# Transposes between a mixer's stages: squares of 32x32 on VectorE in place of whole ones on TensorE

## The reference

```python
h = rms_norm(x, pre_g)
q_a, k_a, v_a, z_a, u_c, b_c, c_c, z_c, q_r, k_r, v_r, z_r, g_a, g_c, g_r = split(h @ w_in)
o_a = dilated_mixture_attn(q_a, k_a, v_a) * silu(z_a)          # 12 heads of 128
o_c = b_c * causal_short_conv(c_c * u_c, conv_w, conv_b) * silu(z_c)   # 1536 channels, 3 taps
o_r = retention(q_r, k_r, v_r) * silu(z_r)                     # 12 heads, q and k rotated
merged = sigmoid(g_a) * (o_a @ w_a) + sigmoid(g_c) * (o_c @ w_c) + sigmoid(g_r) * (o_r @ w_r)
x = x + rms_norm(merged @ w_out, post_g)
```

## Time and profile before

| | |
|---|---|
| median of 3 runs | 2805.48 us (2804.77 to 2805.68) |
| profiled execution | 2805.61 us, span 2803.7 us |
| mean granted clock of TensorE | 0.999 |
| matmuls on TensorE | 12744 |
| ScalarE busy | 1257.4 us, 45% |
| DMA | 189 GB/s in the mean, 56.1% of 16 engines' time; 1 MB of weights lands in 5.1 us |

### The profile page before, as it was taken

One profiled execution on the slowest core, in us unless ns is written; L12 is line 12 of the kernel. 1 busy time (PEld: TensorE's weight loads), 2 busy tenths in 40 slices (PEclk: granted clock), 3 DMA queues, 4 the chain that ended last, 5 costly groups with the idle time before them and its releaser, 6 DMA issues.

```text
span 2803.7 us, 30612 instructions
## 1 busy us (share of the span) xinstructions
PE 2785.3 (99%) x12744; PEld 2318.5 (83%) x12744; DVE 1514.7 (54%) x1663; ACT 1257.4 (45%) x1484; POOL 26.6 (1%) x35
## 2 busy tenths in 40 slices
PE   8999999999999999999999999999999999999998
PEld 7888888888888888888878888888888888888887
DVE  5554544555545666546555445445555556555465
ACT  5554544444443444444455545444444434344443
POOL 0000000000000000000000000000000000000000
PEclk9999999999999999999999999999999999999999
DMA  8555555555656555556565555555655565555563
GB/s 311 167 180 179 172 191 194 192 190 186 195 193 192 171 193 169 176 191 215 181 225 171 176 179 177 191 192 191 193 184 194 195 194 167 192 169 179 194 211 135
DMA packets 264107, 529.13 MB, mean 189 GB/s; under 512 B 8352, under 2 KB 8480, under 8 KB 263712
## 3 DMA queue, kind: packets, MB, share of 16 engines
q1 hardware_dynamic: 260208, 517.24, 56.1%
q10 hardware_dynamic: 2752, 5.05, 0.5%
q0 software_dynamic: 1008, 4.87, 0.5%
HBM read 522.94 MB, written 4.19 MB: 188 GB/s over the span
## 4 chain that ended last, share of the span: by engine, by line
PE 99%; DVE 0%; DMA 0%; ACT 0%; issue 0%; DVEq 0%; POOL 0%; ACTq 0%; POOLq 0%
PE ps L589 32%; PE ps L591 32%; PE ps L590 32%; PE ps L473 2%; PE ps L531 0%; PE ps L528 0%; PE ps L529 0%; PE ps L502 0%; PE ps L506 0%; PE ps L515 0%; DMA merged<-xT 0%; PE ps L507 0%; PE ps L501 0%; DVE gates L1068 0%; DVE hT_trail L1040 0%
## 5 line engine op out<-in xcount | busy, mean ns | idle before, releaser
L836 DVE TENSOR_TENSOR w_trail<-raw,w_lead 128x1024 fp32r<-128x1024 f32 x975 | 1192.0, 1225 | 1250.4 <-ACT w_lead L648 1248.7
L648 ACT ACTIVATE w_lead<-raw 128x1024 fp32r<-128x1024 f32 x975 | 1032.4, 1060 | 1487.2 <-PE ps L591 1479.3
L589 PE MATMUL ps<-w_lead,hT_lead 128*128 128x512 f32 x3328 | 1304.6, 392 | 10.8 <-DVE w_trail L1077 9.3
L591 PE MATMUL ps<-w_lead,hT_trail 128*128 128x512 f32 x3328 | 1296.6, 390 | 0.0
L590 PE MATMUL ps<-w_trail,hT_lead 128*128 128x512 f32 x3328 | 1296.1, 389 | 0.0
L589 PEld LDWEIGHTS ps<-w_lead,hT_lead 128*128 128x128 f32 x3328 | 625.6, 188 | 138.6 <-DVE hT_trail L1059 9.2
L591 PEld LDWEIGHTS ps<-w_lead,hT_trail 128*128 128x128 f32 x3328 | 625.3, 188 | 130.5
L590 PEld LDWEIGHTS ps<-w_trail,hT_lead 128*128 128x128 f32 x3328 | 625.8, 188 | 127.2
L589 PE MATMUL ps<-w_lead,oT_lead 128*128 128x512 f32 x576 | 224.6, 390 | 0.0
L591 PE MATMUL ps<-w_lead,oT_trail 128*128 128x512 f32 x576 | 224.1, 389 | 0.0
L590 PE MATMUL ps<-w_trail,oT_lead 128*128 128x512 f32 x576 | 224.1, 389 | 0.0
(11 more groups left out here) (96 smaller groups left out, 783.9 us busy)
## 6 DMA issues: line engine op xcount, KB each, us to landing
raw<-w_in SPq DMA_DIRECT2D x383, 1024.0 KB, 5.1
raw<-w_out SPq DMA_DIRECT2D x32, 1024.0 KB, 5.1
raw<-w_branch_a SPq DMA_DIRECT2D x24, 1024.0 KB, 5.0
raw<-w_branch_c SPq DMA_DIRECT2D x24, 1024.0 KB, 5.1
raw<-w_branch_r SPq DMA_DIRECT2D x24, 1024.0 KB, 5.0
gates<-x SPq DMA_DIRECT2D x4, 512.0 KB, 13.2
post_gain<-post_norm_g POOLq DMA_DIRECT2D x2, 1024.0 KB, 6.7
gates<-x ACTq DMA_DIRECT2D x4, 512.0 KB, 6.1
```

What stands on the lines that cost most here:

```text
L589: pe.matmul(acc, lead[:, k, tok(t)], wl, start=(k == 0), stop=False)
L591: last = pe.matmul(acc, trail[:, k, tok(t)], wl, start=False, stop=(k == BLOCKS[n][2] - 1))
L648: act.activation(w_lead[:, h % SPLIT_SLOTS, :], raw[:, i % RAW_SLOTS, part:part + HALF * COLS], ACT.Copy).then_inc(lead_ready, 1)
L836: dve.tensor_tensor(w_trail[:, s, :], raw[:, i % RAW_SLOTS, part:part + HALF * COLS], w_lead[:, s, :].bitcast(F32), ALU.subtract).then_inc ...
```

## The change

TensorE's and ScalarE's steps q, k, prod and the transposing part of out go. In their place VectorE turns the 256x512 tile (in SBUF as 128 x 2 x 512) in sixteen instructions, each of 32 partitions x 256 elements: it reads partitions 32i to 32i+31 and writes partitions 32j to 32j+31, eight squares of 32x32 each. They are dealt over six halves (`TURNS`: 3, 3, 3, 3, 2, 2), for q from 2B, for k from 3B, for prod from 2B, for z from the half behind values (attention), gate (conv and retention). The z turn writes `qT`, free by then; out reads it from there. Scores wait for the two turns. The steps behind move by one to six halves, exp from 3B+5 to 3B+7. The first piece of each turn also waits for the trails of the group before. One wait of the branch blocks is counted on `out_trail` in place of three kinds.

```diff
-STEPS = {"attention": TILES + TILES + HPB + HPB + HPB // 2 + TILES,
-         "conv": TILES + TILES,
-         "retention": TILES + TILES + HPB + HPB // 2 + TILES}
+STEPS = {"attention": HPB + HPB + HPB // 2,
+         "conv": 0,
+         "retention": HPB + HPB // 2}
...
+SQ = 32
+QUADS = P // SQ
+TURNS = ((0, 3), (3, 6), (6, 9), (9, 12), (12, 14), (14, 16))
...
+def pieces(what, at):
+    return [(what + str(i), at + i) for i in range(len(TURNS))]
...
 PE_DUE = due({
-    "attention": [("q", 2 * B + 3), ("k", 3 * B + 2), ("scores", 3 * B + 4), ("probs", 4 * B + 2),
-                  ("values", 4 * B + 4), ("out", 4 * B + 6)],
-    "conv": [("prod", 2 * B + 2), ("out", 4 * B + 2)],
-    "retention": [("q", 2 * B + 3), ("k", 3 * B + 3), ("scores", 3 * B + 5), ("values", 4 * B + 1),
-                  ("out", 4 * B + 6)]})
+    "attention": [("scores", 3 * B + 6), ("probs", 4 * B + 4), ("values", 4 * B + 6)],
+    "conv": [],
+    "retention": [("scores", 3 * B + 6), ("values", 4 * B + 2)]})
 ACT_DUE = due({
-    "attention": [("q", 2 * B + 3), ("k", 3 * B + 2), ("exp", 3 * B + 5), ("probs", 4 * B + 2),
-                  ("out", 4 * B + 6)],
-    "conv": [("prod", 2 * B + 2), ("out", 4 * B + 2)],
-    "retention": [("q", 2 * B + 3), ("k", 3 * B + 3), ("square", 4 * B + 1), ("out", 4 * B + 6)]}, AHEAD)
+    "attention": [("exp", 3 * B + 7), ("probs", 4 * B + 4), ("out", 5 * B + 4)],
+    "conv": [("out", 4 * B + 6)],
+    "retention": [("square", 4 * B + 2), ("out", 5 * B + 2)]}, AHEAD)
 DVE_DUE = due({
-    "attention": [("scores", 3 * B + 4), ("sums", 4 * B + 1), ("values", 4 * B + 4), ("out", 4 * B + 6)],
-    "conv": [("conv0", 2 * B + 3), ("conv1", 2 * B + 4), ("conv2", 2 * B + 5), ("gate", 4 * B),
-             ("out", 4 * B + 2)],
-    "retention": [("scores", 3 * B + 5), ("values", 4 * B + 1), ("norm", 4 * B + 2),
-                  ("gate", 4 * B + 3), ("out", 4 * B + 6)]}, AHEAD)
+    "attention": pieces("q", 2 * B) + pieces("k", 3 * B) + [("scores", 3 * B + 6), ("sums", 4 * B + 3),
+                 ("values", 4 * B + 6)] + pieces("z", 4 * B + 7) + [("out", 5 * B + 5)],
+    "conv": pieces("prod", 2 * B) + [("conv0", 2 * B + 6), ("conv1", 2 * B + 7), ("conv2", 3 * B),
+             ("gate", 4 * B)] + pieces("z", 4 * B + 1) + [("product", 4 * B + 6), ("out", 4 * B + 7)],
+    "retention": pieces("q", 2 * B) + pieces("k", 3 * B) + [("scores", 3 * B + 6), ("values", 4 * B + 2),
+                  ("norm", 4 * B + 3), ("gate", 4 * B + 4)] + pieces("z", 4 * B + 5) + [("out", 5 * B + 3)]}, AHEAD)
...
-                if what in ("q", "k"):
-                    i = "qk".index(what)
-                    pe.wait_ge(tables_in, 16)
-                    if mixer == "attention":
-                        pe.wait_ge(*moved_out(l, n0 + 1 + i))
-                    else:
-                        pe.wait_ge(*rotated_tiles(l, TILES * (2 * g + i + 1)))
-                    src = (q_sb, k_sb)[i]
-                    for t in range(TILES):
-                        transposes(l, m + TILES * i + t, [src[:, t, head(h)] for h in range(HPB)])
-                elif what == "prod":
-                    pe.wait_ge(*moved_out(l, n0 + 1))
-                    for t in range(TILES):
-                        transposes(l, m + t, [q_sb[:, t, head(h)] for h in range(HPB)])
-                elif what == "scores":
-                    for i in range(2 * TILES):
-                        pe.wait_ge(*step_drained(l, m + i))
+                if what == "scores":
+                    pe.wait_ge(*turned(l, "q", mixer, g))
+                    pe.wait_ge(*turned(l, "k", mixer, g))
                     for h in range(HPB):
...
+                    pe.wait_ge(tables_in, 16)
...
-                elif what == "out":
-                    s0 = m + STEPS[mixer] - TILES
-                    if mixer == "attention":
-                        for i in range(HPB // 2):
-                            pe.wait_ge(*step_drained(l, s0 - HPB // 2 + i))
-                    elif mixer == "conv":
-                        pe.wait_ge(conv_gated, l * (TILES * GROUPS) + TILES * (g + 1))
-                    else:
-                        pe.wait_ge(ret_gated, l * GROUPS + (g + 1))
-                    for t in range(TILES):
-                        transposes(l, s0 + t, [z_sb[:, t, head(h)] for h in range(HPB)])
 
...
-                    if mixer == "conv":
-                        pe.wait_ge(conv_trail, l * (TILES * GROUPS) + TILES * GROUPS)
-                    else:
-                        s = step0(mixer, GROUPS - 1) + STEPS[mixer] - TILES
-                        for t in range(TILES):
-                            pe.wait_ge(*step_drained(l, s + t))
+                    done = TILES * GROUPS * (MIXERS.index(mixer) + 1)
+                    pe.wait_ge(out_trail, l * (TILES * GROUPS * len(MIXERS)) + done)
...
-                if what in ("q", "k", "prod"):
-                    i = 1 if what == "k" else 0
-                    for t in range(TILES):
-                        s = m + TILES * i + t
-                        dst = prodT[:, :, 2 + t * P:2 + (t + 1) * P] if what == "prod" else (qT, kT)[i][:, :, tok(t)]
-                        act.wait_ge(*step_ready(l, s))
-                        act.activation(dst, heads4(side(s)[:, :]), ACT.Copy).then_inc(drained[s % SIDE_BANKS], 1)
-                elif what == "exp":
+                if what == "exp":
...
                 elif what == "out":
-                    s0 = m + STEPS[mixer] - TILES
+                    if mixer != "conv":
+                        act.wait_ge(*turned(l, "z", mixer, g))
                     for t in range(TILES):
                         dst = oT_lead[:, HPB * g:HPB * (g + 1), tok(t)]
                         if mixer == "conv":
-                            act.wait_ge(*step_drained(l, s0 + t))
-                            act.activation(dst, heads4(work2[:, t, :]), ACT.Copy).then_inc(out_lead, 1)
-                        else:
-                            lead_of_step(l, s0 + t, dst)
+                            act.wait_ge(conv_product, l * (TILES * GROUPS) + TILES * g + t + 1)
+                        act.activation(dst, out_source(mixer, t), ACT.Copy).then_inc(out_lead, 1)
...
-                if what == "scores":
+                if what[:-1] in ("q", "k", "prod", "z"):
+                    turn(l, what[:-1], mixer, g, int(what[-1]))
...
-                        for t in range(TILES):
-                            dve.wait_ge(*step_drained(l, m + t))
+                        dve.wait_ge(*turned(l, "prod", mixer, g))
...
+                elif what == "product":
+                    dve.wait_ge(*turned(l, "z", mixer, g))
+                    dve.wait_ge(conv_steps, l * (3 * HPB * GROUPS) + 3 * HPB * (g + 1))
+                    for t in range(TILES):
+                        dve.tensor_tensor(heads4(work2[:, t, :]), qT[:, :, tok(t)], kT[:, :, tok(t)],
+                                          ALU.mult).then_inc(conv_product, 1)
                 elif what == "out":
-                    s0 = m + STEPS[mixer] - TILES
-                    for t in range(TILES):
-                        s = s0 + t
-                        if mixer == "conv":
-                            dve.wait_ge(*step_ready(l, s))
-                            if t == 0:
-                                dve.wait_ge(conv_steps, l * (3 * HPB * GROUPS) + 3 * HPB * (g + 1))
-                            dve.tensor_tensor(heads4(work2[:, t, :]), heads4(side(s)[:, :]), kT[:, :, tok(t)],
-                                              ALU.mult).then_inc(drained[s % SIDE_BANKS], 1)
                     for t in range(TILES):
                         lead = oT_lead[:, HPB * g:HPB * (g + 1), tok(t)]
                         dst = oT_trail[:, HPB * g:HPB * (g + 1), tok(t)]
-                        if mixer == "conv":
-                            dve.wait_ge(*lead_steps(l, lead_no(mixer, g, t)))
-                            dve.tensor_tensor(dst, heads4(work2[:, t, :]), lead.bitcast(F32),
-                                              ALU.subtract).then_inc(conv_trail, 1)
-                        else:
-                            trail_of_step(l, s0 + t, lead_no(mixer, g, t), lead, dst)
+                        dve.wait_ge(*lead_steps(l, lead_no(mixer, g, t)))
+                        dve.tensor_tensor(dst, out_source(mixer, t), lead.bitcast(F32),
+                                          ALU.subtract).then_inc(out_trail, 1)
+
+            def turn(l, what, mixer, g, piece):
+
+                n0 = first_block(mixer, g)
+                src = {"q": q_sb, "k": k_sb, "prod": q_sb, "z": z_sb}[what]
+                if what == "prod":
+                    dst, done = prodT[:, :, 2:], prod_turned
+                else:
+                    dst, done = {"q": (qT, q_turned), "k": (kT, k_turned), "z": (qT, z_turned)}[what]
+                if piece == 0:
+                    before = l * 3 * GROUPS + group_no[mixer, g]
+                    if before > 0:
```

(52 more changed lines are left out.)

## The result

The changed kernel takes 2790.25 us in the median of 5 runs (2786.76 to 2792.14) against 2805.68 (2804.77 to 2805.90): ratio 0.9944, 95% interval 0.9932 to 0.9955, 15.4 us faster. The forecast was 2784. The runs of the kernel before that were taken beside the experiments have their medians at 2805.31 (the first four experiments) and 2805.18 (the last four); each experiment is compared with those. The profiled execution took 2791.59 us, its span is 2789.7, 14.0 under the one before.

A forecast was written before the change was run, and what follows sets the result against it. TensorE, busy 99% of the span, was taken as the bound. 42 us off for transposes, less 5 (attention's scores), 14 (retention's) and 1 (exp), gives 22 off: 2805.6 - 22 = 2784 us, range 2766 to 2818.

The forecast's parts named there:

- the gain on TensorE: 384 transposes, 48 batches of eight, leave TensorE's queue at 0.87 us each: 42 us off.
- the price of a transpose: One VectorE transpose of 32 partitions x 256 elements takes 0.44 us, between bounds of 0.36 and 0.68.
- d: Time of one VectorE transpose instruction, taken as 0.44 us without overlap, since each changes partitions.
- the filling of a square: 32 elements must be in before a square's first can leave: 0.03 us added to each VectorE transpose.
- Attention's 0.8 us: TensorE waits 0.8 us for the last k piece at attention's scores, six times: 5 us.
- retention's 2.4: TensorE waits 2.4 us at retention's scores, as VectorE rotates k before turning it; six times: 14 us.
- exp's slot: Exp moves into the half evicting z with a Sigmoid; w_trail 0.1 us late, six times: under 1 us.
- z and the product at nothing: The rest of z's and the product's turns cost nothing, hidden by VectorE's idle half; ScalarE's next split about 4 us late.
- rival 3: Retention's six 2.4 us waits each throw TensorE's clock to 1.2 GHz: 14 us of gain lost, 2798; chance 0.06.
- Rival 2: VectorE becomes the bound in retention's q and k blocks: 36 us slower, 2842, deciding from d = 0.59; chance 0.18.
- Starved weights: Rival 2's late w_trail: at d = 0.68 retention's k block loses 0.7 + 2.2 us on weights.

The follow-up runs named there:

- the first four experiments: Retention's scores one half later, 2769.1 us; all scores one half later, 2761.98; only the product and z on VectorE, 2785.16; only q and k there, 2811.78.
- the last four: Squares staying in their partitions, 2777.09 us; four more transposes per k turn, 2813.35; these with all scores one half later, 2772.55; retention's k turn with fourteen, 2779.40.

## Why the prediction was right, and what it lacked

**Right: the gain on TensorE.** 42 us were costed; without any wait 43.3 are measured, so a batch is 0.90 and not 0.87. The prediction had read 0.89 from the starts and took the smaller value.

**Right: the price of a transpose.** d = 0.44 was taken; it lasts 0.436 and starts 0.447 behind the one before. The reason given for no overlap was right as well: partitions change, and where they don't the starts are 0.36 apart. That the last 0.03 is the filling of a square was argued and isn't shown: the same instruction records 414 ns where it overlaps.

**Right: where the waits come.** Attention's 0.8 us was measured as 0.82 of added distance, retention's 2.4 as 2.64. Retention's wait was undersized by 0.24, six times 1.4 us (the sum rounded it to 14, and 15.9 were measured): a half with three pieces takes 2.61 to 2.63 us (936.81 to 939.42 to 942.05), not 2.545, since the first transpose starts 1.25 us behind w_trail and not 1.225, and each transpose leaves 0.01 behind it. Counted from the half's last matmul (946.22 less 2.72 is 943.50) VectorE ended at 5.49 where 5.22 was worked out, and TensorE started 0.11 later where 0.12 was.

**Right: exp's slot.** It ran as worked out (table loads of 1.28 at 103.38 and 105.97, the next split at 110.79). Counted from the half's last matmul at 101.88, w_trail ended at 11.21 where 11.05 stood and TensorE started at 11.26 where it wanted 11.11: late by 0.16 for "0.1". Since the matmul behind it slips too, it is 0.32 a group, in five groups and not six: 1.6 us where "under 1" stood.

**Right: z and the product at nothing.** ScalarE is 4.1 us late at z's last piece where "about 4" stood.

**What it lacked: the clock, which it held apart as rival 3.** The prediction gave the clock 0.06 and let it happen to all six waits or none, on the argument that waits of 0.5 us don't lower it. It happens to some: four of six in one profile, three of six in another, at the same 2.88 us of distance. It costs 1.6 to 1.7 us each and not 2.4; the lower level lasted for the scores (1.28 us for a head, 949.92 to 951.20, in place of 0.66) and little longer. That is 6.5 us of the profiled execution. The scores behind a wait, 1.0 in all, had no term either. From the forecast's 22 to the measured 14 it goes so: 1.3 more for the batches, 0.5 more at the start, 6.5 less for the clock, 1.9 less for retention's wait, 1.0 for those scores and 0.6 more than the 1 us set aside for exp: 22 + 1.8 - 10.0 = 13.8. That the forecast came as near as 6 us owes a little to luck, as the batches, costed 1.3 too low, nearly hid what exp and the first scores took. The runs' own spread goes with the clock: the three of 2790.25 to 2792.14 have a mean clock of 0.997, the two of 2786.76 and 2787.15 have 0.999.

**Rival 2 lies a little nearer than it was put.** With k turns of 20 transposes (as if d were 0.56 there) the kernel is already 8 us slower than before; the prediction put the point at 0.59. The clock is the difference: six slow scores at 2.2 us are 13 us, more than the 8, so without it this run would still be faster than the kernel before. What turned the sign was the scores' wait with the clock behind it, not late weights. Starved weights, the rest of that rival, weren't reached by any run.

Open: at what distance between 2.0 and 2.9 us the clock begins to fall wasn't tried, nor why it falls in one group and not in the next.

## What to carry to other kernels

Before moving work from the bounding engine to an idle one, look not at the idle share but at the consumer: here VectorE was 46% idle, and what decided was one half between the last piece of k and the scores. A due time is a free term of such a change; moving it by one half, with exp behind it, nearly tripled the gain (15 to 43 us). And a wait on TensorE can cost more than its length: of the 28 us regained some 6 were the clock's. Nor does a list of waits show all: 0.16 us for late weights stood in none, and with what followed it cost 1.6 us; it shows only in the distances between starts.

## What the runs showed of the hardware

- A float32 transpose of 32 partitions x 256 elements on VectorE lasts 436 ns, and starts 0.447 us behind another when partitions change. When they stay it starts 0.36 behind and lasts 414 ns.
- The clock behind a gap ahead of the scores, from one matmul's start to the next, over all profiles: 0.9 to 1.05 us, never lower (30 gaps); 1.6 to 2.0 us, never (24); 2.88 us, lower in seven of twelve, each 1.6 to 1.7 us dear over the scores and the two halves behind them; 4.67 us, lower in six of six, 1.7 to 3.0 us dear.
